# Three blocks in one launch on one NeuronCore: the FFN of the second block unrolled, with its convolution taps read from the PSUM banks; the last expert closes its own sums; the bias table is stored by SP in sixteen transfers

## What is computed

```python
def second_block(x, ...):
    ...
    h = rmsnorm(x, ffn_pre_norm[l])
    up = causal_dwconv(h @ w_ffn_up[l], ffn_conv_w[l], ffn_conv_b[l])   # (256, 6144), 3 taps
    f_gate, f_val = jnp.split(up, 2, axis=-1)
    f = (jax.nn.gelu(f_gate, approximate=True) * f_val) @ w_ffn_down[l]
    x = x + rmsnorm(f, ffn_post_norm[l])

def swa_attention(q, k, v, sinks, rel_bias):       # third block; moba_attention uses the same table
    ...
    bias = rel_bias[t5_bucket(dist)]               # 8 heads, distances 0..382
```

## Time and profile before

| | |
|---|---|
| median of three runs | 2014.65 us (2014.63 to 2015.08) |
| profiled execution, its own time | 2014.23 us |
| its span, first to last instruction | 2012.4 us |
| PE busy | 1537.4 us (76%) |
| PE weight load busy | 1036.4 us (51%) |
| VectorE busy | 715.4 us (36%) |
| ACT busy | 593.5 us (29%) |
| HBM read over the span | 564.89 MB, 283 GB/s |

### The profile page before, as it was taken

One profiled execution on the slowest core, in us unless ns is written; L12 is line 12 of the kernel. 1 busy time (PEld: TensorE's weight loads), 2 busy tenths in 40 slices (PEclk: granted clock), 3 DMA queues, 4 the chain that ended last, 5 costly groups with the idle time before them and its releaser, 6 DMA issues.

```text
span 2012.4 us, 25017 instructions
## 1 busy us (share of the span) xinstructions
PE 1537.4 (76%) x10341; PEld 1036.4 (51%) x10341; DVE 715.4 (36%) x1136; ACT 593.5 (29%) x1009; POOL 96.3 (5%) x44
## 2 busy tenths in 40 slices
PE   4999886565666666566556569999879999898897
PEld 2787731111111111111111139989869888797897
DVE  3347320000000000000000028767667885558564
ACT  4443420000000000000000025765644553455453
POOL 1264300000000000000000000000000000000000
PEclk8999887888887878877788889999989998899899
DMA  9366559999999999999999983344554443443230
GB/s 402 135 251 243 240 242 427 429 429 428 429 429 428 429 428 429 429 429 428 428 429 428 429 350 143 134 147 148 161 150 164 174 155 138 157 150 133 85 126 22
DMA packets 48439, 570.10 MB, mean 283 GB/s; under 512 B 4592, under 2 KB 10736, under 8 KB 11888
## 3 DMA queue, kind: packets, MB, share of 16 engines
q1 hardware_dynamic: 40992, 556.81, 67.4%
q10 hardware_dynamic: 7376, 12.29, 2.5%
HBM read 564.89 MB, written 4.19 MB: 283 GB/s over the span
## 4 chain that ended last, share of the span: by engine, by line
PE 44%; DMA 39%; DVE 11%; ACT 3%; issue 2%; DVEq 1%; ACTq 1%; POOL 0%; SPq 0%
PE bank L1488 44%; DMA ring<-in_w_down 13%; DMA ring<-in_w_gate 12%; DMA ring<-in_w_up 12%; DVE ring_rounded L2078 2%; ACT work L1796 1%; DVE work L899 1%; DMA ring<-in_w_ada 1%; DVE rstd L2024 1%; ACT weights_high_rounded L1796 1%; DVE h_normed L2028 1%; DVE work L2028 1%; ACTq L660 1%; DVE work L895 0%; POOL ring_rounded L1473 0%
## 5 line engine op out<-in xcount | busy, mean ns | idle before, releaser
L1488 PE MATMUL bank<-ring,work 128*32 128x512 f32 x3008 | 481.2, 772 | 315.2 <-DMA ring<-in_w_up 126.4
L1796 ACT ACTIVATE work<-bank 128x256 f32<-128x256 f32 (+4 forms) x291 | 128.9, 453 | 1136.2 <-PE bank L1488 812.0
L1488 PEld LDWEIGHTS bank<-ring,work 128*32 128x32 f32 x3008 | 92.8, 125 | 671.3 <-DMA ring<-in_w_up 208.1
L2078 DVE TENSOR_TENSOR ring_rounded<-ring,weights_high_rounded 128x1024 fp32r<-128x1024 f32 x208 | 250.3, 1221 | 117.5 <-ACT weights_high_rounded L1796 117.4
L1796 ACT ACTIVATE weights_high_rounded<-ring 128x1024 fp32r<-128x1024 f32 x244 | 255.7, 1052 | 22.0 <-PE bank L1488 21.9
L2248 DVE TENSOR_TENSOR work<-work,bank 128x512 f32<-128x512 f32 x16 | 16.5, 1030 | 594.4 <-PE bank L1488 594.4
L1488 PE MATMUL bank<-h_high_rounded,weights_high_rounded 128*128 128x256 f32 x1296 | 202.1, 296 | 19.0 <-ACT h_high_rounded L1796 17.7
L1488 PEld LDWEIGHTS bank<-h_high_rounded,weights_high_rounded 128*128 128x128 f32 x1296 | 172.7, 194 | 36.6 <-issue 23.6
L1488 PE MATMUL bank<-h_high_rounded,ring_rounded 128*128 128x256 f32 x1296 | 181.1, 283 | 12.5 <-DVE ring_rounded L2078 12.0
L1488 PE MATMUL bank<-h_normed_rounded,weights_high_rounded 128*128 128x256 f32 x1296 | 181.3, 284 | 0.0
L1488 PEld LDWEIGHTS bank<-h_high_rounded,ring_rounded 128*128 128x128 f32 x1296 | 164.5, 193 | 15.7 <-DVE ring_rounded L2078 14.4
(11 more groups left out here) (225 smaller groups left out, 1168.2 us busy)
## 6 DMA issues: line engine op xcount, KB each, us to landing
ring<-in_w_down SPq DMA_DIRECT2D x64, 2048.0 KB, 16.3
ring<-in_w_gate SPq DMA_DIRECT2D x63, 2048.0 KB, 16.4
ring<-in_w_up SPq DMA_DIRECT2D x61, 2048.0 KB, 16.3
ring<-in_dense SPq DMA_DIRECT2D x60, 2048.0 KB, 8.0
ring<-in_w_ada SPq DMA_DIRECT2D x12, 2048.0 KB, 12.7
work<-in_w_up SPq DMA_DIRECT2D x3, 1024.0 KB, 13.3
bias_diagonals<-work ACTq DMA_DIRECT2D x2, 1532.0 KB
ring<-in_dense SPq DMA_DIRECT2D x2, 1024.0 KB, 18.8
```

Source lines behind the costliest of these rows:

```text
L1488: return nc.tensor.matmul(o, lhsT, rhs, start=start, stop=stop)
L1796: return nc.scalar.activation(o, i, f, **kw)
L2078: v.tensor_tensor(as_r(w), w, w_high[:, buffer, :], ALU.subtract).then_inc(s.w_low, 1)
```

## The change

Three edits. First, the FFN's up part is unrolled on all engines: ACT's copy becomes an Identity activation with the weight of tap 2 as scale and the bias, written to the tile's final place; VectorE's taps 1 and 0 read the bank; PE waits with the reuse of a bank for the second of these taps (`conv_step`); GELU, product and split follow one pair behind. Second, the last expert is written out after the loop and its matmuls close the sums, and the eight matmuls (four in the code) that closed them are gone. Third, SP stores the table, in sixteen transfers of 128 whole rows of 384 floats, each from one partition, between the load of block 19 and that of block 20; ACT fills the two last columns; the wait for the stored table moves from VectorE's FFN start to ACT's copy of unit 40 of the FFN.

```diff
@@ tensor_block2
-            tensor_loop2(pe, dense_unit, L_UP, 3, normed, IN_AT["up"][0])
+            for u in range(2 * FT):
+                if u >= 4:
+                    pe.wait_ge(s.conv_step, taps_through(u - 4))
+                unit2(L_UP + u, normed, None if u else "up")
+            pe.wait_ge(s.conv_step, taps_through(2 * FT - 1))
@@ scalar_block2
                 if n == 3:
+                    fn(TW[0:AH, :, TOEP:TPITCH], ones[0:AH, 0:2].unsqueeze(2), ACT.Copy).then_inc(s.toep_sb, 1)
                     for kind in range(2):
                         act.wait_ge(s.toep_mm, kind + 1)
                         fn(TW[0:AH, kind, 0:TOEP], B[4 + kind][0:AH, 0:TOEP], ACT.Copy).then_inc(s.toep_sb, 1)
-                    act.wait_ge(s.toep_sb, 2)
-                    for kind in range(2):
-                        act.dma_start(d["toep"][kind * AH:(kind + 1) * AH, :, 0:TOEP],
-                                      spread(TW[0:AH, kind, 0:TOEP], 1, P)).then_inc(s.toep_stored, 16)
...
-            scalar_loop2(act, fn, units_done, L_UP, 1)
-            scalar_loop2(act, fn, units_done, L_UP + ROUND, 2, activate)
...
+            for u in range(2 * FT):
+                unit_done(d2_block(L_UP + u), block_ends(L_UP + u))
+                if u == 40:
+                    act.wait_ge(s.toep_stored, 32 * AH)
+                fn(ffn_conved(u), B[(PU2 + L_UP + u) % 4][:, 0:SEQ], ACT.Identity, scale=ffn_weight(u, 2),
+                   bias=par("ffn_conv_b", u, u + 1)).then_inc(s.dense_sb, 1)
+                weight_high(D1_UNITS + L_UP + u + AHEAD2)
+                k = u // 2
+                if u % 2:
+                    act.wait_ge(s.conv_step, taps_through(u - 1))
+                    fn(FV[:, k, :], FV[:, k, :], ACT.Gelu_apprx_tanh).then_inc(s.ffn_gelu, 1)
+                elif k:
+                    split_high(UP[:, 2 * (k - 1), :], FV[:, k - 1, :])
+            split_high(UP[:, 2 * (FT - 1), :], FV[:, FT - 1, :])
@@ vector_block2
-            dve.wait_ge(s.toep_stored, 32)
...
+            for k in range(FT):
+                for u in (2 * k, 2 * k + 1):
+                    tap(u, 1)
+                    weight_low(L_UP + u + AHEAD2)
+                    tap(u, 2)
+                    if u % 2 == 0 and k:
+                        split_low(FV[:, k - 1, :], UP[:, 2 * (k - 1), :])
+                dve.wait_ge(s.ffn_gelu, k + 1)
+                dve.wait_ge(s.conv_step, taps_through(2 * k + 1))
+                v.tensor_tensor(FV[:, k, :], FV[:, k, :], UP[:, 2 * k, :], ALU.mult).then_inc(s.act_full, 1)
@@ sync
-            with sp.Fori(0, D2_BLOCKS // RING) as r:
+            rounds_before = (L_SSM + 4) // (RING * UNITS) + 1
+            with sp.Fori(0, rounds_before) as r:
+                dense2_round(r)
+            sp.wait_ge(s.toep_sb, 3)
+            for kind in range(2):
+                for h in range(AH):
+                    sp.dma_start(d["toep"][kind * AH + h:kind * AH + h + 1],
+                                 spread(TW[h:h + 1, kind, :], 1, P)).then_inc(s.toep_stored, 16)
+            with sp.Fori(rounds_before, D2_BLOCKS // RING) as r:
+                dense2_round(r)
@@ tensor, experts
-            with pe.Fori(1, EXPERTS) as e:
+            with pe.Fori(1, EXPERTS - 1) as e:
                 expert(e)
-            for q in range(4):
-                last = mm(B[4 + q][:], ZERO[0:1, 0:P], ZERO[0:1, :], False, True)
-            last.then_inc(s.acc_done, 1)
+            expert(EXPERTS - 1, final=True)
```

More of the change, by code:

```diff
@@ L387, in conv_unit, with taps_through, ffn_weight, ffn_conved @@
             return dst, par(name + "_w", 4 * n, 4 * n + 4), par(name + "_b", n, n + 1)
+        def taps_through(u):
+            return 2 * u + 2
+        def ffn_weight(u, tap):
+            return par("ffn_conv_w", 3 * u + tap, 3 * u + tap + 1)
+        def ffn_conved(u):
+            return tiles(u - 1, 1) if u % 2 else tiles(48 + u // 2, 1)
         def tensor_block2(pe, mm, dense_unit, column_sum, column_sums):
@@ L504, in tensor_block2, with scalar_block2 @@
             column_sum(8, KT - 1)
[L506 to L527, removed]
+        def scalar_block2(act, fn, link, square, squares_of_x, root_table, root, unit_done, weight_high, split_high):
             def copy2(unit, dst, tile=None):
@@ L926, in vector_block2, with tap @@
[L926 to L932 removed]
+            def tap(u, shift):
+                o = ffn_conved(u)
+                if shift == 1:
+                    dve.wait_ge(s.dense_sb, PU2 + L_UP + u + 1)
+                else:
+                    dve.wait_ge(s.conv_step, taps_through(u) - 1)
+                v.scalar_tensor_tensor(out=o[:, shift:SEQ], in0=B[(PU2 + L_UP + u) % 4][:, 0:SEQ - shift],
+                                       scalar=ffn_weight(u, 2 - shift), in1=o[:, shift:SEQ],
+                                       op0=ALU.mult, op1=ALU.add).then_inc(s.conv_step, 1)
@@ L1491, in arrived, with dense_unit @@
                 pe.wait_ge(ring_loaded[block_no % RING], uses(block_no))
-            def dense_unit(block_no, sub, bank, high, low, counts, base=None, first=True, last=True, turn=None):
+            def dense_unit(block_no, sub, bank, high, low, counts, base=None, first=True, last=True):
                 buffer = w_high[:, (counts - 1) % HIGHS, :]
-                if turn is not None:
-                    counts = turn + counts
                 parts = [("hh", buffer, high), ("lh", None, high), ("hl", buffer, low)]
@@ L1716, in _, with expert @@
             pe.wait_ge(s.xs_sb, KT)
-            def expert(e):
+            def expert(e, first=False, final=False):
                 def expert_block(b):
-                    if isinstance(e, int):
+                    if first:
                         if b in EXTRA:
@@ L1739, in expert @@
                                           k == 0, k == KT - 1)
-                        if not (isinstance(e, int) and 4 * half + b in EXTRA):
+                        if not (first and 4 * half + b in EXTRA):
                             last.then_inc(s.ring_used, 1)
@@ L1986, in _ @@
                 weight_high(D1_UNITS + unit)
-            scalar_block2(act, fn, link, square, squares_of_x, root_table, root, unit_done, units_done, weight_high, split_high, splits_passed)
+            scalar_block2(act, fn, link, square, squares_of_x, root_table, root, unit_done, weight_high, split_high)
             scalar_block3(act, fn, link, squares_of_x, root_table, root, unit_done, weight_high, split_high)
```

92 lines of the change are left out of this document (10 added, 82 removed).

## The result

The changed kernel takes 2050.89 us (median of four, 2049.6 to 2051.89) against 2014.87 us for the kernel before on the same chips: a ratio of 1.0176, 95% interval 1.0158 to 1.0194. It is 36 us slower. The forecast was 2070, its range 2032 to 2082, with 0.80 on slower. The profiled execution of the changed kernel has a span of 2049.9 us, 37.5 more than before.

A forecast was written before the change was run, and what follows sets the result against it. PE was taken to bound the second half wherever fed, VectorE leading in the FFN from about 1580. From 2014.23 us, +79.2 for the late block 20, -18.4 FFN and -3.7 closing matmuls gave 2071.3; forecast 2070, range 2032 to 2082.

The forecast's parts named there:

- the likeliest case: SP's table store reads one four-partition share at a time, as forecast: 2070 us, range 2055 to 2082, chance 0.71.
- the second rival: Table store: 33.2 packets per us for all sixteen engines, or some run ahead; 62 to 110 us, time 2010 to 2058, chance 0.10.
- Length of the store: SP's 2048 table rows, read from one partition at a time at 16.6 packets per us, would last 123 us.
- the old store was even to its end: ACT's store in the kernel before stayed even among its engines, taken as evidence against engines running ahead; no size given.
- SP issues at 0.33 us each, 5 us in all: Issuing the sixteen table transfers on SP would take 5 us in all and not be the limit.
- From the last packet to the FFN: Block 20 lands 6.2 us after the store's end; high weights, square, column sums and root then take 10.6 us.
- FFN, gain 18.4: Unrolled FFN up part: PE leads at 2.80 us a unit, through the down part's first tile; gain 18.4 us, bounds 14 to 20.
- The 1.7 us for a halved clock: Down part's first tile: estimated 1.7 us extra for a halved TensorE clock behind PE's wait for the last taps.
- the low weight covers the taps' dependence: FFN up part: VectorE's low weight between two taps hides their dependence, giving 4.7 us per pair against PE's 5.6.
- Closing matmuls, 3.7: After the last expert: removing 8 closing matmuls with nothing beside them gains 3.7 us.
- ACT's 9.2 us: Ahead of the FFN: ACT no longer held issuing the table's store gains 9.2 us alone, used up if block 20 is late.
- The quick rival: SP's table store: packet time belongs to each engine, so sixteen need 31 us and block 20 is in time; 1983 us, chance 0.16.

The follow-up runs named there:

- experiments 4 and 5: Changed kernel's sixteen one-partition transfers: in 4 read from partitions 16 apart, 2006.75 us; in 5 only the heads reordered 0, 4, 1, 5, 2, 6, 3, 7, 2009.16 us.
- experiment 1: Changed kernel with the table's store back on ACT in its old form, the other two edits kept: 1989.74 us.
- experiment 2: Changed kernel with SP's store in two transfers of eight partitions each, same place in the queue: 2007.98 us.
- experiment 3: Changed kernel with the table made on 128 partitions and stored by SP in two transfers, same packets and place in the queue: 1978.45 us.
- the measure of 8: The changed kernel with the table on 128 partitions, run again as the base for two FFN edits: 1977.35 us.
- experiment 8: Two FFN edits, each alone on the changed kernel with a 128-partition table: low weights behind both taps, 1973.93 us; down part's waits by bank, 1975.36 us.
- experiment 6: Kernel before the change with only the table on 128 partitions, still stored by ACT: 2004.12 us.
- the second edit of experiment 8: Changed kernel with a 128-partition table, PE's one wait for all taps before the down part replaced by one per bank: 1975.36 us.

## Why the prediction was right, and which terms were mis-sized

**Place and mechanism were right.** ACT's high weights of unit 80 wait for block 20, behind the store in SP's queue, and the FFN starts late. I had it at 1584.8 less 3.7 for the experts, 1581.1; it was 1564.19, 16.9 us sooner. The time, 2050.89, lies in the range of 2032 to 2082, but 4 us below the 2055 that the likeliest case had for its lower end; only the second rival took the range further down.

**Length of the store, 123 us: 19 too long.** The price of one transfer was nearly right: 7.18 us in the chain, against 128 / 16.6 = 7.7. Sixteen of them are 115. What I left out is the change of group. The engines don't keep step. At a change those that are ahead read group 4 to 7 while the others still read 0 to 3, and 53 to 67 GB/s flow. Three changes save some 10.6 us, the difference between 115 and 104.3. The packet records bear this out: in 1466 to 1474, 1492 to 1500 and 1514 to 1524 there are 38, 68 and 90 packets more than the 17.8 per us of one group, worth 11.0 us together, and nearly none elsewhere. The second rival had this mechanism ("some engines run ahead into the other share's partitions") and the time lies in its 2010 to 2058; so the outcome is the likeliest case with a part of that rival. That the old store was even to its end, which I held against it, says nothing on this. It ran at 33 packets per us from its start, so it never had to drift apart to read both groups. Its packet records speak for engines that stay with one group: in the stretches without weight loads nearly every packet lasts 0.21 to 0.23 us while all eight work, and between 1509.5 and 1511, when some have finished, packets of 0.11 to 0.12 and of 0.22 us stand side by side. The records don't name the engines, so this is argued. The Trainium skill, "SBUF — State Buffer", section "Door 1: The DMA port swizzle", gives a port 27.2 GB/s and puts partitions 0 to 3 on one and 4 to 7 on another; the chain's 27.4 GB/s and experiments 4 and 5 agree. By its figure alone the store would be 116 us, which leaves out the same overlap.

**Issue, "SP issues at 0.33 us each, 5 us in all": wrong, without a price.** SP was held 93.11 us, 7.18 for each transfer, which fits a queue that takes only some three ahead (22.7 us from issue to landing, by the page's list of issues). Block 20 was issued at 1533.66, 12 us before the store ended, and still came right behind it.

**From the last packet to the FFN.** Block 20 came 7.4 us behind it (forecast 6.2), and the first matmul 11.1 behind that (10.6). Together 1.7 us.

**FFN, gain 18.4: 20.3 measured,** 20.7 in experiment 1. (In the working, 1514.3 + 47 x 2.8 is 1645.9, not 1645.6, and so the tile's end 1659.1 or so, not 1658.9; the 18.4 goes with the right sum.) The units run at 2.80 us to the last, and the wait ahead of the down part is 3.25 (3.0). The 1.7 us for a halved clock behind it didn't come: the first eight matmuls took 1.20 us. In experiments 2, 3 and 5 and in the measure of 8 they took 2.07 to 2.08 behind the same wait, with the clock granted at 0.50, and the down part's first squares came 2.5 to 2.7 us later than in the changed kernel (19.62 to 19.84 us behind its first matmul, not 17.14). So the term exists and is then larger than 1.7, but it isn't in every profile; why, these runs don't show. VectorE idles 8.4 us in 11.5 pairs, 0.7 a pair, where I had 0.9. My reason that the low weight covers the taps' dependence is true and unimportant (experiment 8).

**Closing matmuls, 3.7: 3.64,** and alone 4.4, 2.6 to 6.2.

**ACT's 9.2 us** were used up by the late block, as said. Where the block comes in time they are there: 1989.74 - 1978.45 = 11.3 between experiments 1 and 3, 10.5 in experiment 6, by medians. The lowered clock behind the hold, 1.8 us in experiment 6, may be in what is above 9.2; the spread of the runs doesn't show it.

**Sum.** Store -19.1, landing and norm +1.7, start of the store and experts +0.5, FFN -1.9, and 0.7 less in the third block, which I can't tell from the spread of runs: -19.5 against the 2071.3 worked out, which is 2051.8; the profiled execution took 2051.7.

**The quick rival** (1983, chance 0.16) took the 0.216 us of a packet for a price of each engine and got a store of 31 us. Experiment 3 refutes the price: 0.069 us with the same packets, once the engines don't read the same few partitions. The 0.08 and 0.10 us that I held against this rival pointed the right way. That a short store brings out the rest of the gain was right: 1978.45 in experiment 3.

## What to carry to other kernels

Before a store or a load is moved or reshaped, count over how many partitions its SBUF side spreads at any one time, not how many engines it gets: sixteen engines on the same four partitions only waited for each other, and if the transfer must read few partitions, follow each with one from another group. What stands behind it in the same queue pays for its whole length, so compare the length with the slack of the next load (33 us here) before putting it there. A producer that can write the same rows on all partitions for almost nothing (a matmul with repeated columns, and ACT's two copies take 0.86 us for 128 partitions and 0.83 for 8, and the copy that repeats the columns 0.31) can be worth more than any place in a queue.

## What the runs showed of the hardware that was not expected

- Reading four neighbouring partitions alone runs at 27.4 GB/s with sixteen engines at it, and eight engines on two such groups get 51 GB/s. Of the 106 packets in 1482 to 1487, 12 are of 4 bytes and don't belong to the table; the other 94 took 0.940 x 16 x 5 / 94 = 0.80 us each, where the same packets took 0.069 us from 128 partitions.
- Issuing a transfer costs little (1.33 us for two of 1024 rows) where the queue drains fast; where it drains slowly, the engine that issues is held at the rate at which it drains (10.8 us on ACT, 93 us on SP).
- PE's rate at a granted clock of 1.00 isn't the same in all profiled executions. In 40 us of the fed FFN, 1590 to 1630, experiment 3 did 346 matmuls, and the same kernel in the measure of experiment 8 did 338, a unit in 2.86 us instead of 2.80, which over 48 units is 3 us. From the FFN's first matmul to the end of the last unit there are 139.7 to 140.5 us in seven of the ten profiles with the unrolled FFN, and 143.5 to 143.6 in the other three (experiment 2, and the measure and the second edit of experiment 8). The two windows of 40 us, experiment 3 first:

```profile
1590.00:1630.00 40.00, 40.00 (x346) 40.00 (x345) 34.12 (x58) 26.04 (x44) 0.00 (x0) 1.00 0.48 167
```

```profile
1590.00:1630.00 40.00, 40.00 (x338) 40.00 (x337) 33.84 (x56) 25.38 (x43) 0.00 (x0) 1.00 0.50 187
```

Differences of that size between two profiles are not to be read as the effect of an edit.
